# Up projection with the activations standing and the weights moving, and attention values one chunk later

## The reference, cut to what matters

```python
# first block, differential attention: 4 heads, two maps each, 2 x 128 tokens per head
s = jnp.einsum('bqhcd,bkhcd->bhcqk', qi, k) * scale
p = jax.nn.softmax(s, axis=-1)
p = p[:, :, 0] - lam * p[:, :, 1]
o = jnp.einsum('bhqk,bkhe->bqhe', p, v)
...
# first block, MLP: w_up is 2048 x 8192, w_down is 8192 x 2048
h = rms_norm(x, norm_mlp_pre[l])
u = jnp.square(jax.nn.relu(jnp.einsum('bsd,df->bsf', h, w_up[l])))
x = x + rms_norm(jnp.einsum('bsf,fd->bsd', u, w_down[l]), norm_mlp_post[l])
```

## Time and profile before

| what | value |
|---|---|
| median of 3 runs | 1953.23 us (1952.76 to 1953.46) |
| the profiled execution | 1952.63 us |
| its span in the profile | 1950.7 us |
| TensorE busy | 1936.4 us, 99% |
| VectorE busy | 1255.6 us, 64% |
| ScalarE busy | 962.1 us, 49% |
| DMA queue of SP | 396.76 MB, 64.1% of 16 engines' time |

### The profile page before, as it was taken

How to read it: one execution, slowest core, us unless ns; L and a number is a source line. 1 busy time by engine, 2 the same in 40 slices (tenths; PEclk the granted TensorE clock), 3 DMA queues, 4 the chain that set the end, 5 groups by cost and what they waited for, 6 DMA issues and landing times.

```text
span 1950.7 us, 22705 instructions
## 1 busy us (share of the span) xinstructions
PE 1936.4 (99%) x9222; PEld 1625.9 (83%) x9222; DVE 1255.6 (64%) x1231; ACT 962.1 (49%) x892; POOL 17.8 (1%) x31
## 2 busy tenths in 40 slices
PE   9999999999999999999999999999999999999998
PEld 7888888888888888888888888888889888888886
DVE  7747647745666655455566666677588868676665
ACT  6344434445445444444455555565555546544444
POOL 0000000000000000000000000000000000000000
PEclk9999999999999999999999999999999999999999
DMA  9876977775867376666665555566578554546763
GB/s 320 257 231 174 265 241 216 232 242 193 254 208 257 114 210 189 193 182 187 184 196 192 192 193 192 192 214 213 173 207 256 187 171 153 183 173 221 215 216 108
DMA packets 326392, 399.79 MB, mean 205 GB/s; under 512 B 131212, under 2 KB 154512, under 8 KB 325648
## 3 DMA queue, kind: packets, MB, share of 16 engines
q1 hardware_dynamic: 325272, 396.76, 64.1%
q10 hardware_dynamic: 1016, 1.59, 0.2%
HBM read 381.00 MB, written 17.31 MB: 204 GB/s over the span
## 4 chain that ended last, share of the span: by engine, by line
PE 91%; DVE 4%; issue 3%; ACT 2%; POOL 0%; ACTq 0%; POOLq 0%; DVEq 0%
PE acc L1544 79%; PE mis L1544 12%; ACT hi L575 1%; DVE m L952 1%; DVE lo L970 1%; PE mis L1547 1%; DVE m L960 0%; ACT at L604 0%; DVE at L1004 0%; ACT m L565 0%; POOL st L513 0%; DVE sm L960 0%; ACT m L564 0%; DVE st L1048 0%; DVE st L956 0%
## 5 line engine op out<-in xcount | busy, mean ns | idle before, releaser
L1544 PE MATMUL acc<-hi,at 128*128 128x512 f32 (+1 forms) x4384 | 1358.5, 389 | 0.4 <-DVE lo L970 0.3
L970 DVE TENSOR_TENSOR lo<-raw,hi 128x2048 fp32r<-128x2048 f32 (+1 forms) x333 | 752.9, 2263 | 506.2 <-ACT hi L575 505.0
L1544 PEld LDWEIGHTS acc<-hi,at 128*128 128x128 f32 x4384 | 819.7, 188 | 165.2 <-DVE lo L970 1.0
L575 ACT ACTIVATE hi<-raw 128x2048 fp32r<-128x2048 f32 (+1 forms) x333 | 628.7, 1891 | 503.1 <-PE acc L1544 422.0
L1544 PE MATMUL acc<-lo,at 128*128 128x512 f32 (+1 forms) x2192 | 845.8, 386 | 0.0
L1544 PEld LDWEIGHTS acc<-lo,at 128*128 128x128 f32 x2192 | 411.6, 188 | 80.8 <-DVE lo L980 0.3
L1544 PE MATMUL mis<-at,hi 128*128 128x512 f32 x512 | 139.7, 394 | 0.0
L1544 PE MATMUL acc<-at,hi 128*128 128x512 f32 x448 | 122.3, 394 | 0.0
L1544 PEld LDWEIGHTS mis<-at,hi 128*128 128x128 f32 x512 | 88.0, 189 | 12.4
L952 DVE TENSOR_TENSOR m<-m 128x256 f32<-128x256 f32 (+1 forms) x145 | 75.0, 518 | 20.4 <-ACT m L564 15.7
L1544 PEld LDWEIGHTS acc<-at,hi 128*128 128x128 f32 x448 | 77.0, 189 | 10.9
(11 more groups left out here) (134 smaller groups left out, 686.0 us busy)
## 6 DMA issues: line engine op xcount, KB each, us to landing
raw<-in_w_in SPq DMA_DIRECT2D x133, 1024.0 KB, 5.2
raw<-in_w_up SPq DMA_DIRECT2D x64, 1024.0 KB, 5.4
raw<-in_w_down SPq DMA_DIRECT2D x64, 1024.0 KB, 5.1
raw<-in_w_out SPq DMA_DIRECT2D x32, 1024.0 KB, 5.1
raw<-in_w_pg SPq DMA_DIRECT2D x16, 1024.0 KB, 5.2
m<-turned SPq DMA_DIRECT2D x21, 512.0 KB, 5.8
raw<-in_w_in SPq DMA_DIRECT2D x12, 688.0 KB, 4.9
raw<-in_w_a SPq DMA_DIRECT2D x8, 1024.0 KB, 5.2
```

What stands on the lines that cost most here:

```text
L575: e.activation(hi_of(n), raw_of(n), ACT.Copy).then_inc(s_hi.on("hi", n))
L970: e.tensor_tensor(lo, raw, hi.bitcast(F32), ALU.subtract).then_inc(s_lo.on("lo", n))
L1544: return e.matmul(o, a, b, start=start, stop=stop)
```

## The change

Up blocks 1 to 15 are done as block 0 is: `products` in place of `columns`, Relu with the scale and Square on ACT into US, the transposes on DVE, eight block DMAs and one load on SP. US is one buffer, the transposed blocks alternate between two places. The scale tile RB, its matmuls and its copy go. The values of the attention (and all that follows them: normalisation, their turn, SP's transfers of them) come one chunk later, at 28 + v.

```diff
-            plan("upw" if j else "up", j, w_up, 0, 16, 512 * j, 512, "r1")
+            plan("up", j, w_up, 0, 16, 512 * j, 512, "r1")
...
-        for u in range(11):
+        for u in range(12):
             beside(24 + u, "da", u)
...
-        beside(N_UP + 4, "rb")
-        for j in range(1, 16):
-            beside(N_UP + 4 * j + 4, "ut", j, 1)
...
-        turns_of[("ut", 0)] = N_UP + 5
+        turns_of.update({("ut", j): N_UP + 4 * j + 5 for j in range(16)})
...
# SP
-                u, v = n - 31, n - 34
+                u, v = n - 31, n - 35
...
-                u, v = n - 30, n - 33
+                u, v = n - 30, n - 34
...
# ACT
-                if i % 16:
-                    ac.wait_ge(s_act, "ut", i % 16, 1)
-                else:
-                    ac.wait_ge(loaded("heads", ("ut", 0)), "heads", ("ut", 0))
+                ac.wait_ge(loaded("heads", ("ut", i % 16)), "heads", ("ut", i % 16))
...
-                if 0 <= u - 3 < 8:
-                    v = u - 3
+                if 0 <= u - 4 < 8:
+                    v = u - 4
...
                     if kind == "up":
                         ac.wait_ge(s_pool, "r1")
+                        if j:
+                            ac.wait_ge(s_dve, "turned", ("ut", j - 1), t)
                         act(US[:, t, :], ps[t], ACT.Relu, scale=ST[:, 52 + t:53 + t]).then_inc(s_act.on("evac", b, t))
-                        act(US[:, t, :], US[:, t, :], ACT.Square).then_inc(s_act.on("up sq", t))
+                        act(US[:, t, :], US[:, t, :], ACT.Square).then_inc(s_act.on("up sq", j, t))
...
# DVE
-                if own in ("mix", "pg") and i == 2:
-                    dv.wait_ge(loaded("blocks", (own, 0)), "blocks", (own, 0))
+                if own in ("mix", "ut", "pg") and i >= 2:
+                    dv.wait_ge(loaded("blocks", (own, i - 2)), "blocks", (own, i - 2))
...
-                if kind == "upw":
-                    z, u = column_banks(j), UX[j % 2]
-                    dv.wait_ge(s_act, "low sums", j)
-                    tt(u, z[:, :, 0:S], u, ALU.add).then_inc(s_dve.on("evac", b, 1))
-                    dv.wait_ge(s_act, "rb")
-                    stt(u, u, 0.0, RB.unsqueeze(1).broadcast_to([P, 4, S]), ALU.max, ALU.mult).then_inc(s_dve.on("up rows", j))
-                    return
...
# TensorE
-                    if blocks[chunks[n][2]][0] == "upw":
-                        if t == 1:
-                            columns(n)
-                    elif chunks[n][5] != "p":
+                    if chunks[n][5] != "p":
                         products(n, t)
```

More of the change, by code:

```diff
@@ L153, in program @@
         US = t2(64, 512)
-        UX = [m(a, 1024).rearrange("p (c s) -> p c s", c=4) for a in (68, 72)]
-        RB = m(76, 256)
         VM = M[:, 0:2056].rearrange("p (t h c) -> p t h c", t=2, h=4)
@@ L235, in program @@
         number = {(kind, j): b for b, (kind, j, n, ids) in enumerate(blocks)}
-        on_dve = ("rope", "upw", "a", "b", "wo", "z", "g", "res")
+        on_dve = ("rope", "a", "b", "wo", "z", "g", "res")
         def stage(name, g, t):
             return STG[name][(g if name in ("r1", "r2") else 2 * g + t) % 2]
-        def column_banks(j):
-            return mis if j % 2 else acc
         def freed(b):
@@ L354, in turned_to @@
                 own, g = j
-                return m({"mix": 24 + 4 * (g % 2), "ut": 68, "pg": 48 + 4 * (g % 2)}.get(own, 4 * g) + 2 * t, 512)
+                return m({"mix": 24 + 4 * (g % 2), "ut": 68 + 4 * (g % 2), "pg": 48 + 4 * (g % 2)}.get(own, 4 * g) + 2 * t, 512)
             return TURNED[(2 * (j if j < 4 else j - 2) + t) % 8]
@@ L361, in heads_of @@
                     return m((32 if j[0] == "mix" else 16) + 4 * j[1], 1024).rearrange("p (h s) -> p h s", h=4)
-                z, j = {"hf": HB, "qk": QKR, "hq": HQ, "ut": UT}[j[0]], j[1]
+                if j[0] == "ut":
+                    return UT[:, 4 * j[1]:4 * j[1] + 4, :]
+                z, j = {"hf": HB, "qk": QKR, "hq": HQ}[j[0]], j[1]
             else:
@@ L664, in sig @@
                     act(v, v, ACT.Sigmoid).then_inc(s_act.on("sig", g))
[L666 to L672, removed]
             def turn_v(j):
@@ L779, in evac @@
                 ps = [acc[:, 2 * (b % 2) + t, 0:n] for t in range(2)]
-                if kind == "upw":
-                    ac.wait_ge(s_prod, "products", ids[-1], 1)
-                    act(UX[j % 2], column_banks(j)[:, :, S:2 * S], ACT.Copy).then_inc(s_act.on("low sums", j))
-                    return
                 for t in range(2):
@@ L879, in finish @@
                     e.dma_start(o_d[:, t, slice(*PIECES[1])], XS[:, t, slice(*PIECES[1])]).then_inc(s_out2.on("out", t), 16)
-            do = dict(lam=lam, da=da, na=na, sig=sig, ut=ut, rb=rb, cut=cut, bounds=bounds, forget=forget, conv=conv, gate=gate,
+            do = dict(lam=lam, da=da, na=na, sig=sig, cut=cut, bounds=bounds, forget=forget, conv=conv, gate=gate,
                       turn_v=turn_v, hg=hg, ml=ml, p_parts=p_parts)
@@ L1077, in turn @@
                     dv.wait_ge(loaded("blocks", ("qk", i)), "blocks", ("qk", i))
-                if own in ("mix", "pg") and i == 2:
-                    dv.wait_ge(loaded("blocks", (own, 0)), "blocks", (own, 0))
+                if own in ("mix", "ut", "pg") and i >= 2:
+                    dv.wait_ge(loaded("blocks", (own, i - 2)), "blocks", (own, i - 2))
                 for t in range(2):
                     if own == "ut":
-                        dv.wait_ge(s_act, "up sq", t)
+                        dv.wait_ge(s_act, "up sq", i, t)
                     elif own in ("hd", "hf", "qk", "hq"):
@@ L1611, in products @@
                 if k == 0 and b >= 2:
-                    pe.wait_ge(freed(b - 2), "evac", b - 2, 1 if blocks[b - 2][0] == "upw" else t)
+                    pe.wait_ge(freed(b - 2), "evac", b - 2, t)
                 for j in range(4):
@@ L1622, in products @@
                 r.then_inc(s_prod.on("products", n, t))
[L1624 to L1665, removed]
             def first():
@@ L1850, in turnover @@
                     products(c, 1)
-            do = dict(x_sums=x_sums, da=da, na=na, rb=rb, gate=gate, turn_v=turn_v, hg=hg, ml=ml)
+            do = dict(x_sums=x_sums, da=da, na=na, gate=gate, turn_v=turn_v, hg=hg, ml=ml)
             turn[0] = 0
```

## The result

The changed kernel takes 1939.28 us (median of 4 runs, 1938.87 to 1939.40) against 1953.32 us before (4 runs). The ratio is 0.9929, with a 95% interval of 0.9918 to 0.9941: 14.0 us, 0.7% faster.

The account below looks back on a forecast made before the run. TensorE, busy 1936.4 of 1950.7 us, was taken as the bound. Up projection -10.8, attention waits -2.4 and one more change of work +0.05 gave -13.1 us, so 1953.23 became 1940.1 us; 8-in-10 range 1938.3 to 1943.2 us.

Parts of the forecast that it names:

- the attention term: Attention stretch: values one chunk later remove TensorE's three waits, 2.37 us, less 0.05 us for one more change of work.
- TensorE in the up stage: Up blocks 1 to 15: 60 chunks at 5.44 us instead of 5.61, 326.4 against 337.21 us, 10.8 us less.
- The third rival: Up projection: only the number of columns counts, new chunks stay at 5.61 us; 1950.5 us, chance 0.03.
- ACT and DVE in the up stage: Up blocks: ACT's 2.1 us become at most 2.8, neither engine comes near 21.8 us a block; cost nothing.
- SP and DMA: Up blocks: eight issues and a load per turn cost nothing; a turn takes 3.0 us of all 16 engines, DMA share 0.78.
- The 8.9 us to spare: Up blocks: margin claimed in every block for the weight load behind the turn's writes before TensorE would wait.
- the slower rival: Up blocks: SP's queue delays weights until TensorE waits; gain gone at a 17.6 us landing, 1974.6 us at 19; chance 0.04.
- DVE's margin: Attention, low part of chunk 34: after the change it would be ready 0.2 us before TensorE needs it, thin but positive.
- The first rival: Attention gives nothing back, DVE's lag replacing the waits at chunks 33 to 35; 1942.4 us, chance 0.12.
- the second: Up stage: each of 15 block boundaries loses 0.05 to 0.2 us, 0.8 to 3 us in all; 1940.9 to 1943.1 us, chance 0.08.

Follow-up runs that it names:

- turn_writes_x2: Changed kernel with each small write of the turn in up blocks 1 to 15 issued twice, the additional ones to scratch tensors; 1959.9 us.
- x2_over_two_steps: `turn_writes_x2` with the doubled writes split by token halves over two SP steps, a weight load between them; 1957.5 us.
- turn_writes_x3: Changed kernel with each small write of the turn in up blocks 1 to 15 issued three times, the additional ones to scratch tensors; 2032.4 us.

## Why the prediction was right, and where not

1939.28 us lie in its range of 1938.3 to 1943.2, 0.8 us from the 1940.1 forecast; 0.7 of these are the attention term, below.

**TensorE in the up stage**: right, 10.8 us forecast and 10.8 measured, alone (11.1 by the medians) and together. The third rival, that only columns count, is out: a chunk is 5.44 us. The reason given, eight more and shorter matmuls, holds for 0.13 of the 0.17 us; for the other 0.04 no cause was found. The Trainium skill ("TensorE: Matmul & The Clock Gate", "Back-to-back issue gap") gives N / 2.4 + 2.5 ns for the isolated gap, and for a sustained stream of weight loads and matmuls some 131 ns at 512 columns. The trace agrees with neither: 226.7 ns at 512 columns in both forms, which is N / 2.4 + 13.4, and among mixed widths 231 to 236 ns at 512 and 115 to 119 at 256 (N / 2.4 + 8 to 12).

**ACT and DVE in the up stage**: right. ACT is busy 155.77 / 15 = 10.4 us and DVE 10.7 us in a block, and neither makes TensorE wait.

**SP and DMA**: right that they cost nothing, wrong in two sizes. The 8.9 us to spare were wrong: I followed a load forward to its use and did not close the loop that goes from its low part over DVE's order to the next turn's writes. The runs show 1.6 to 3 us. The break-even of the slower rival, a landing of 17.6 us, was far too generous: with twice the writes the kernel is slower than before (1959.9 us) though no load took more than 12.6 us to land. And a turn costs 0.85 x 21.76 - 0.62 x 22.45 = 4.6 us of the 16 engines, not 3.0. The earlier trace rows stopped at 696.71 us, while the turned rows were read back only from 693.41 us on; the next stretch of the kernel before, which has no turn of its own, shows the rest:

```profile
696.71:719.16 22.45, 22.45 (x129) 19.62 (x129) 11.53 (x6) 9.64 (x6) 0.00 (x0) 1.00 0.70 224
```

(0.70 - 0.62) x 22.45 = 1.8 us more, and 3.0 + 1.8 = 4.8. That this term came out at nothing was in part luck: the same working passed twice the writes as well, and those cost 20.6 us.

**Attention**: the mechanism right, the term too small. All three waits were those of the probabilities' load, and DVE's margin came out at 0.3 us where 0.2 was forecast. The wait was sized by the idle time shown (2.37 us) instead of by the distances (3.0 us), so 2.35 us were forecast, net of the 0.05, and 3.0 measured. The first rival did not occur. Nor did the second, a loss at each turn: four chunks take 21.76 us with the boundary of a block among them.

## What to carry to other kernels

Where TensorE is the bound, count matmuls and not only columns: cutting the same columns into more and shorter pieces cost 0.13 us a chunk here, 8 us over the stage, while which operand stands still was free at 512 columns. To price a queue's burst, close the loop in which it lies (here writes, load, split, next turn, next writes) and compare it with the period; what lies between a load and its use is only a buffer that can be spent once. And take a stall's worth from start to start of the instructions around it, because pipelined matmuls hide part of the gap.

## What the runs showed of the hardware

The time for which a DMA issue holds SP is not its own. Sixteen issues of 64 KB took 11.8 us in `turn_writes_x2`, and half as many took the same 11.8 us in `x2_over_two_steps`, right behind two 1 MB loads; single issues of these writes held SP for 0.33 to 2.77 us in the up stage of the changed kernel.

TensorE's granted clock fell where it had kept waiting. The mean over the execution is 0.983 with three times the writes, where TensorE waits up to 7.3 us at a time, and 0.996 with twice. Busy times by stretch of `turn_writes_x2` (two of its stretches) and of `turn_writes_x3`:

```profile
872.40:875.80 3.40, 3.40 (x9) 2.66 (x9) 2.69 (x2) 2.69 (x2) 0.00 (x0) 0.51 0.97 270
964.60:968.00 3.40, 3.40 (x9) 2.62 (x10) 2.83 (x3) 2.74 (x2) 0.00 (x0) 0.50 0.85 213
```

```profile
760.00:860.00 100.00, 85.66 (x347) 69.30 (x346) 38.39 (x21) 36.93 (x31) 0.00 (x0) 0.92 0.83 211
```

The first two ran at 1.2 in place of 2.4 GHz: 9 matmuls in 3.4 us, where 15 fit at 0.2267 us. They begin right behind the two longest waits for a low part, of 2.15 us to 871.41 us and of 2.39 us to 964.43 us; the shorter ones of that stage were not followed by a fall. In the third, a mean of 0.92 means that part of it ran at the lower clock.

With this the 20.6 us of `turn_writes_x2` can be estimated from rows: 14.0 us of shown waits, 12 x 0.23 = 2.8 us that the shown idle time leaves out (0.16 + 0.07 us a pause, as in the attention), and half of the 6.8 us at the lower clock, 3.4 us, are 20.2 us. Near its bound a kernel pays more for a wait than the wait.
